# Up products of a feed-forward stage: high and low activations in one matmul of 512 columns, in two halves of a PSUM bank

## The chip, the cores and the metric

One core of one Trainium2 chip runs the whole program. The metric is the device time of one launch in microseconds. Engines are named as in the profile: PE is TensorE (PEld its loads of the stationary operand), DVE is VectorE, ACT is ScalarE, POOL is GpSimd, SP is SyncE.

## What is computed

Two blocks of two layers each on a sequence of 256 tokens with 1024 features. The change touches only the feed-forward part of the first block's layers:

```
def conv_glu_ffn(x, w_up, w_conv, w_down):
    u = causal_dwconv(x @ w_up, w_conv)
    gate, up = jnp.split(u, 2, axis=-1)
    return (jax.nn.silu(gate) * up) @ w_down
...
        h = h + mixed @ w_out[l]
        h = h + conv_glu_ffn(rms_norm(h, norm_ffn[l]), ffn_up[l], ffn_conv[l], ffn_down[l])
```

`w_up` is 1024 x 5632, `w_down` 2816 x 1024, `causal_dwconv` has three taps a column.

## The kernel before, in words

Activations lie transposed, features on the 128 partitions and the 256 tokens along the free dimension. Weights stream from HBM in slabs of 128 x 2048 float32 (1 MB), one slab to a unit of work; three slab buffers and three pairs of split weights rotate. Every product is made from three float32r products: a value is split in a high part (rounded by ScalarE, `act_round`, L566) and the low rest (subtracted by VectorE, `dve_split`, L904), for weights (`w_high`, `w_low`) and activations (`act_high` = `xh`, `act_low` = `xl`) alike, and `gemm` (L1379 to L1384) issues high x high, high x low and low x high, 256 columns each, into the same columns of a PSUM bank.

The order of the work is a list of units (`UNITS_A`) which `woven` turns into one sequence of steps that all engines walk, each doing its own part of a step. Before unit u, ScalarE rounds and VectorE splits the slab of unit u + 2. Round u + 2 waits until the products of unit u - 1 are done, since it writes the same buffer. TensorE begins a unit when `slab_split` has counted its slab.

The feed-forward part has 22 ups and 11 downs. An up (kind `up`, number j) makes one 128-row tile of the gate half and one of the up half: 2 tiles x 8 depths x 3 matmuls = 48. A down takes two hidden tiles into eight output tiles, also 48 matmuls, and adds into banks 3 to 6 over all 11. The order is up 0 to up 5, down 0, up 6, up 7, down 1, and so on to up 20, up 21, down 8, down 9, down 10 (`ffn_units`, `LAG_DOWN = 2`). Ahead of it stand the four `out` units (attention and mixer results into the residual). Up 0 runs for six depths over the end of that, between the sums of squares of the new norm (`sum`, L1494) on TensorE; its factor per token is spread over partitions by one matmul in bank 7 (`pe_spread`, L1538) and copied by ScalarE into the row `ROW_` (`norm` in `scalar_a`, tally `row_kept`).

What `ffn(j)` does for up j on the two other engines is where the change is. On VectorE (`vector_a`): multiply the bank by the row into `UP_` (L1012, which frees the bank, tally `dve_emptied`), multiply silu(gate) by the up half of j - 1 (L1019, `hidden`), take the low part of hidden tile j - 2 (L1004), then, once ScalarE has made the newest tap, add the other two taps of both halves in four dependent operations (L1031). On ScalarE (`scalar_a`): silu of j - 1, high part of hidden j - 2, then the newest tap of both halves from `UP_` (L632 is the helper that records all of these). `Line.settled()` makes an engine wait for its own last operation, `Banks.fill` makes TensorE wait until a bank has been read.

Banks 0, 1 and 2 rotate among the units, one for an up; bank 7 belongs to norms and transposes. The plan is made by a program (`plan`), which counts who empties which bank how often.

## Time and profile before

| | |
|---|---|
| median of 3 runs | 1706.5 us (1704.61, 1706.5, 1706.65) |
| the profiled execution | 1709.35 us |
| its span | 1707.5 us |
| PE busy | 1678.2 us (98% of the span), 13048 matmuls |
| DVE busy | 1165.8 us (68%) |
| ACT busy | 941.9 us (55%) |
| POOL busy | 194.4 us (11%) |
| HBM read | 264.42 MB, 156 GB/s |
| mean granted clock of PE | 0.991 |

The profiled execution is one run on the chip; its 1709.35 us enclose the span, with 1.85 us around it. Shares are of the span. A busy engine is one with at least one instruction in flight; matmuls overlap each other. Line numbers (L1012) are those of the kernel before.

### The profile page before, as it was taken

How to read it: one execution, taken by the hardware profiler on the slowest of the kernel's cores; microseconds unless marked ns; L12 is line 12 of the kernel's file. 1: busy time of each engine (PE TensorE's matmuls, PEld its weight loads, DVE VectorE, ACT ScalarE, POOL GpSimd, SP SyncE). 2: the span in 40 equal slices, each digit the busy share in tenths (PEclk: the TensorE clock that was granted, in tenths of full speed). 3: DMA queues.
4: the chain of work that ended last, by engine and by line, in shares of the span. 5: the costliest groups of instructions: out<-in, count | busy, mean ns of one | idle time of the engine just before them, and what ended most of it. 6: DMA issues, size and time to landing. Idle time of an engine off the chain costs nothing.

```text
span 1707.5 us, 30908 instructions
## 1 busy us (share of the span) xinstructions
PE 1678.2 (98%) x13048; PEld 1533.8 (90%) x13048; DVE 1165.8 (68%) x1627; ACT 941.9 (55%) x1386; POOL 194.4 (11%) x208
## 2 busy tenths in 40 slices
PE   7999999999999999999999999999999999999998
PEld 6989999999998989999999998887888988878887
DVE  7877556787778975548887775656766646567664
ACT  5584425554555574335554555665774556657742
POOL 0454500000001655200000000000000100000000
PEclk9999999999999999999999999999999999999998
DMA  6433533454544424434455554344345453443451
GB/s 226 168 136 105 172 115 124 176 192 176 189 176 168 171 82 137 156 121 168 158 197 180 180 191 168 128 142 162 141 158 187 166 204 124 147 161 137 163 182 50
DMA packets 48058, 268.25 MB, mean 157 GB/s; under 512 B 13553, under 2 KB 14449, under 8 KB 16177
## 3 DMA queue, kind: packets, MB, share of 16 engines
q1 hardware_dynamic: 38448, 264.70, 43.8%
q8 instruction: 104, 1.70, 0.4%
q10 hardware_dynamic: 8704, 0.53, 0.3%
q0 software_dynamic: 768, 1.05, 0.3%
q14 instruction: 34, 0.27, 0.0%
HBM read 264.42 MB, written 1.84 MB: 156 GB/s over the span
## 4 chain that ended last, share of the span: by engine, by line
PE 88%; DVE 7%; ACT 3%; POOL 1%; issue 1%; DMA 0%; SPq 0%; POOLq 0%; DVEq 0%; ACTq 0%
PE bank L1382 14%; PE bank L1383 14%; PE bank L1384 14%; PE bank L2475 10%; PE bank L2477 10%; PE bank L2476 10%; DVE w_low L904 2%; PE bank L2505 2%; ACT arena L632 1%; PE bank L1619 1%; PE bank L2546 1%; PE bank L1620 1%; PE bank L1621 1%; PE bank L2493 1%; DVE arena L1130 1%
## 5 line engine op out<-in xcount | busy, mean ns | idle before, releaser
L904 DVE TENSOR_TENSOR w_low<-slab,w_high 128x2048 fp32r<-128x2048 f32 x250 | 585.2, 2345 | 243.9 <-ACT w_high L566 236.4
L1382 PE MATMUL bank<-act_high,w_high 128*128 128x256 f32 x2304 | 660.1, 287 | 0.1
L1383 PE MATMUL bank<-act_low,w_high 128*128 128x256 f32 x2304 | 652.0, 283 | 0.0
L1384 PE MATMUL bank<-act_high,w_low 128*128 128x256 f32 x2304 | 651.8, 283 | 0.0
L566 ACT ACTIVATE w_high<-slab 128x2048 fp32r<-128x2048 f32 x250 | 474.0, 1897 | 154.1 <-PE bank L2477 88.3
L1382 PEld LDWEIGHTS bank<-act_high,w_high 128*128 128x128 f32 x2304 | 441.9, 192 | 9.0 <-issue 5.9
L1383 PEld LDWEIGHTS bank<-act_low,w_high 128*128 128x128 f32 x2304 | 442.2, 192 | 0.7 <-issue 0.5
L1384 PEld LDWEIGHTS bank<-act_high,w_low 128*128 128x128 f32 x2304 | 442.0, 192 | 0.0
L2475 PE MATMUL bank<-w_high,act_high 128*128 128x512 f32 x768 | 306.3, 399 | 0.0
L2477 PE MATMUL bank<-w_low,act_high 128*128 128x512 f32 x768 | 300.9, 392 | 0.0
L2476 PE MATMUL bank<-w_high,act_low 128*128 128x512 f32 x768 | 300.2, 391 | 0.0
L2477 PEld LDWEIGHTS bank<-w_low,act_high 128*128 128x128 f32 x768 | 144.7, 188 | 31.0
L2475 PEld LDWEIGHTS bank<-w_high,act_high 128*128 128x128 f32 x768 | 145.0, 189 | 29.8 <-issue 1.3
L2476 PEld LDWEIGHTS bank<-w_high,act_low 128*128 128x128 f32 x768 | 145.1, 189 | 28.4
L2036 POOL TENSOR_TENSOR arena<-arena 128x512 f32<-128x512 f32 x9 | 14.7, 1632 | 1318.6 <-ACT arena L581 1318.5
L632 ACT ACTIVATE arena<-bank 128x512 f32<-128x512 f32 (+2 forms) x96 | 47.8, 520 | 133.5 <-PE bank L1384 39.0
L632 ACT ACTIVATE arena<-arena,vectors 128x256 f32<-128x256 f32 x88 | 40.0, 502 | 121.8 <-DVE arena L1012 121.8
L2108 ACT ACTIVATE arena<-bank,small 128x512 f32<-128x512 f32 x80 | 54.8, 685 | 79.4 <-PE bank L2477 78.4
L1031 DVE SCALAR_TENSOR_TENSOR arena<-arena,vectors 128x255 f32<-128x255 f32 (+1 forms) x176 | 85.2, 484 | 13.4 <-ACT arena L632 5.1
L2108 ACT ACTIVATE arena<-arena,small 128x256 f32<-128x256 f32 (+1 forms) x128 | 56.8, 445 | 40.5 <-DVE small L2335 40.5
L632 ACT ACTIVATE act_high<-arena 128x256 fp32r<-128x256 f32 (+1 forms) x68 | 32.6, 482 | 51.3 <-DVE arena L1085 29.4
L632 ACT ACTIVATE arena<-bank,vectors 128x256 f32<-128x256 f32 x64 | 26.4, 472 | 48.8 <-PE bank L1384 48.3
(239 smaller groups left out, 1711.6 us busy)
## 6 DMA issues: line engine op xcount, KB each, us to landing
slab<-stream_a SPq DMA_DIRECT2D x144, 1024.0 KB, 4.8
slab<-stream_b SPq DMA_DIRECT2D x104, 1024.0 KB, 4.8
residual<-x_t SPq DMA_DIRECT2D x4, 256.0 KB, 5.5
lora_weights<-lora SPq DMA_DIRECT2D x2, 512.0 KB, 8.0
out_t<-residual SPq DMA_DIRECT2D x4, 256.0 KB, 2.2
d_inverse<-arena POOLq DMA_DIRECT2D x2, 256.0 KB, 2.7
constants<-common SPq DMA_DIRECT2D x1, 384.0 KB, 9.6
slab<-stream_a SPq DMA_DIRECT2D x2, 160.0 KB, 6.1
```

The lines of the kernel that those rows point to most:

```text
L566: line.did(eng.activation(core.wh[u % PARTS][:, 0:SLAB_WIDTH[u]], core.slab[u % SLABS][:, 0:SLAB_WIDTH[u]], ACT.Copy), core.sem("slab_high"))
L632: line.did(eng.activation(out, in_, func, **kw), tally)
L904: line.did(line.eng.tensor_tensor(core.wl[u % PARTS][:, 0:SLAB_WIDTH[u]], core.slab[u % SLABS][:, 0:SLAB_WIDTH[u]], core.wh[u % PARTS][:, ...
L1031: did(stt(out=out[:, lag:T], in0=src[:, 0:T - lag], scalar=col("conv", 2 * FT * tap + half * FT + j), in1=out[:, lag:T], op0=ALU.mult, op1 ...
L1382: eng.matmul(out, wh, xh, start=first, stop=False, skip_group_check=True)
L1383: eng.matmul(out, wh, xl, start=False, stop=False, skip_group_check=True)
L1384: return eng.matmul(out, wl, xh, start=False, stop=last, skip_group_check=True)
L2108: line.did(eng.activation(out, in_, func, **kw), tally)
L2475: mm(bank[b][:], high, wh[:, k, :], start=(half == 0 and k == 0), stop=False, skip_group_check=True)
L2476: mm(bank[b][:], low, wh[:, k, :], start=False, stop=False, skip_group_check=True)
L2477: last = mm(bank[b][:], high, wl[:, k, :], start=False, stop=(half == 1 and k == 3), skip_group_check=True)
L2505: ins = mm(core.pair[:, p * BLOCK:][:, SPAN[m]], qk[rows_, m * P:m * P + P], qk[rows_, T:T + WIDTH[m]], start=True, stop=True, skip_group_ ...
```

## The change

All ups are made otherwise. The high and low activations become one tensor `act` of [128, 2, 16, 256]. A wide matmul with the stationary tile `w_high` moves both parts of one depth, 512 columns, and writes them side by side into a whole bank; a second matmul, of 256 columns, adds `w_low` x high to the left half. Gate and up tile now have a bank each, so that an up uses two banks: 0 and 1 for even j, 2 and 7 for odd j, and the ups no longer take part in the rotation of banks 0 to 2. Behind it ScalarE copies the right halves of both banks (256 columns each) into the arena at `REST_`, VectorE adds them to the left halves, and then multiplies the sum by the row in place. ScalarE waits for that product before the newest tap. Downs, branch and out units keep `gemm`.

```
@@ -180,8 +180,8 @@
-        self.xh = sb("act_high", [P, 16, T], F32R)
-        self.xl = sb("act_low", [P, 16, T], F32R)
+        self.x = sb("act", [P, 2, 16, T], F32R)
+        self.xh, self.xl = self.x[:, 0], self.x[:, 1]
@@ -195,8 +195,10 @@
-        first, self.pair, self.pair2 = [bank(f"bank{i}") for i in range(3)], bank("bank3", 1024), bank("bank5", 1024)
-        self.bank = first + [pair[:, 512 * i:512 * i + 512] for pair in (self.pair, self.pair2) for i in range(2)] + [bank("bank7")]
+        self.wide = {0: bank("bank0", 1024), 2: bank("bank2", 1024)}
+        self.pair, self.pair2 = bank("bank3", 1024), bank("bank5", 1024)
+        self.bank = [pair[:, 512 * i:512 * i + 512] for pair in (self.wide[0], self.wide[2], self.pair, self.pair2) for i in range(2)]
+        self.bank.append(self.bank.pop(3))
@@ -244,10 +246,14 @@
-        parts = 1 + i if kind in ("q", "w") else 4 if (kind, i) == ("down", FT // 2 - 1) else max(fills, 1)
+        parts = 1 if kind == "up" else 1 + i if kind in ("q", "w") else 4 if (kind, i) == ("down", FT // 2 - 1) else max(fills, 1)
+        if kind == "up":
+            b = 2 * (i % 2)
+            freed[b, reader] = freed.get((b, reader), 0) + 1
+            banks, fills = [(b, reader, freed[b, reader])], 0
...
@@ -685,7 +691,10 @@
                 eng.wait_ge(*sem("products").upto(rows[UA["down", (j - 10) // 2]][3]))
             act(core.xh[:, 8 + (j - 2) % 8, :], core.a(HID_ + (j - 2) % 4)[:, 0], ACT.Copy, sem("hidden_high"))
         if j < FT:
-            emptied(core, eng, rows, UA["up", j])
+            made(core, eng, rows, UA["up", j])
+            rest = core.wide[rows[UA["up", j]][4][0][0]][:].rearrange("p (j n t) -> p j n t", j=2, n=2)[:, :, 1]
+            act(core.a(REST_ + 2 * (j % 2), 2), rest, ACT.Copy, sem("rest_copied"))
+            eng.wait_ge(*sem("up_scaled").next(eng))
             for half in range(2):
                 act(core.a(CV_ + 2 * (j % 2) + half)[:, 0], core.a(UP_ + 2 * (j % 2) + half)[:, 0], ACT.Identity,
                     sem("newest_tap") if half else None, scale=vec[:, VA["conv"] + 4 * FT + half * FT + j:][:, 0:1])
@@ -1009,7 +1018,12 @@
             if j == 0:
                 eng.wait_ge(*sem("row_kept").next(eng))
             b = rows[UA["up", j]][4][0][0]
-            did(tt(core.a(UP_ + 2 * (j % 2), 2), heads(bank[b], T), over(flat(core, ROW_), 2), ALU.mult), sem(f"dve_emptied{b}"))
+            up = core.a(UP_ + 2 * (j % 2), 2)
+            parts = core.wide[b][:].rearrange("p (j n t) -> p j n t", j=2, n=2)
+            eng.wait_ge(*sem("rest_copied").next(eng))
+            did(tt(up, parts[:, :, 0], core.a(REST_ + 2 * (j % 2), 2), ALU.add), sem(f"dve_emptied{b}"))
+            line.settled()
+            did(tt(up, up, over(flat(core, ROW_), 2), ALU.mult), sem("up_scaled"))
         if 1 <= j <= FT:
             i = j - 1
             eng.wait_ge(*sem("silu").next(eng))
@@ -1423,6 +1437,32 @@
+    def up_banks(u):
+        b = rows[u][4][0][0]
+        return b, {0: 1, 2: 7}[b]
+    def wide_product(u, j, k):
+        wh, wl = (w[(first + u) % PARTS][:].rearrange("p (k j m) -> p k j m", k=8, j=2) for w in (core.wh, core.wl))
+        at, out = inputs["up"](rows[u][1], k), core.bank[up_banks(u)[j]]
+        eng.matmul(out[:].rearrange("p (n t) -> p n t", n=2), wh[:, k, j, :], core.x[:, :, at, :], start=k == 0, stop=False,
+                   skip_group_check=True)
+        return eng.matmul(out[:, 0:T], wl[:, k, j, :], core.xh[:, at, :], start=False, stop=k == 7, skip_group_check=True)
+    def up(u, steps):
+        if steps[0] == (0, 0):
+            eng.wait_ge(sem("slab_split").sem, first + u + 1)
+            b, partner = up_banks(u)
+            banks.free(partner)
+            banks.fill(b, "dve")
+            banks.held[partner] = banks.held[b]
+        for j, k in steps:
+            last = wide_product(u, j, k)
+        if steps[-1] == (1, 7):
+            last.then_inc(sem("products").sem, 1)
@@ -1467,7 +1507,7 @@
-            by_depth(u, range(6))
+            up(u, [(j, k) for k in range(6) for j in range(2)])
@@ -1477,8 +1517,11 @@
-        if (kind, i) in (("br2", 0), ("out", 0), ("up", 0)):
-            return by_depth(u, range(6, 8) if u in begun else range(8 // len(rows[u][4])))
+        if kind == "up":
+            return up(u, [(j, k) for k in range(6 * (u in begun), 8) for j in range(2)] if i == 0 else
+                      [(j, k) for j in range(2) for k in range(8)])
+        if (kind, i) in (("br2", 0), ("out", 0)):
+            return by_depth(u, range(8 // len(rows[u][4])))
```

TensorE at the entry of the first layer's feed-forward part, before: `bank0` to `bank2` are the rotating banks, `bank7` the norms' bank; the rows in between are more matmuls of the same kinds.

```order
L1494 MATMUL bank7<-constants,arena 128x1 [waits gathered,dve_emptied7]
L1494 MATMUL bank7<-constants,arena 128x1 x3
L1382 MATMUL bank1<-act_high,w_high1 128x256 [waits x_ready,dve_emptied1,slab_split]
L1383 MATMUL bank1<-act_low,w_high1 128x256
L1384 MATMUL bank1<-act_high,w_low1 128x256
...
L1538 MATMUL bank7<-arena,constants 128x256 [waits rooted_sums,diagonal]
L1382 MATMUL bank2<-act_high,w_high2 128x256 [waits dve_emptied2,slab_split]
L1383 MATMUL bank2<-act_low,w_high2 128x256
L1384 MATMUL bank2<-act_high,w_low2 128x256
```

The same place in the changed kernel, where `bank0` is the tensor of banks 0 and 1 and `bank2` that of banks 2 and 7:

```order
L1537 MATMUL bank2<-constants,arena 128x1 [waits gathered,dve_emptied7]
L1537 MATMUL bank2<-constants,arena 128x1 x3
L1449 MATMUL bank0<-act,w_high1 128x512 [waits dve_emptied0,x_ready,dve_emptied1,slab_split]
L1451 MATMUL bank0<-act,w_low1 128x256
...
L1581 MATMUL bank2<-arena,constants 128x256 [waits rooted_sums,diagonal]
L1449 MATMUL bank2<-act,w_high2 128x512 [waits dve_emptied2,row_kept,slab_split]
L1451 MATMUL bank2<-act,w_low2 128x256
```

Three matmuls have become two. Up 0 waits for bank 0 as well, which was read last in unit out 3 (`dve_emptied0`), and up 1 waits for `row_kept`, ScalarE's copy of the spread norm out of bank 7.

VectorE in up 2 (one split of a slab, then `ffn(2)`), before:

```order
L904 TENSOR_TENSOR w_low2<-slab2,w_high2 128x2048 [waits dve_steps,slab_high]
L1012 TENSOR_TENSOR arena<-bank0,arena 128x512 [waits products]
L1019 TENSOR_TENSOR arena<-arena 128x256 [waits silu]
L1004 TENSOR_TENSOR act_low<-arena,act_high 128x256 [waits hidden_high]
L1031 SCALAR_TENSOR_TENSOR arena<-arena,vectors 128x255 [waits hidden_low,newest_tap]
L1031 SCALAR_TENSOR_TENSOR arena<-arena,vectors 128x254 [waits dve_steps]
L1031 SCALAR_TENSOR_TENSOR arena<-arena,vectors 128x255 [waits dve_steps]
L1031 SCALAR_TENSOR_TENSOR arena<-arena,vectors 128x254 [waits dve_steps]
```

And in the changed kernel:

```order
L913 TENSOR_TENSOR w_low2<-slab2,w_high2 128x2048 [waits dve_steps,slab_high]
L1024 TENSOR_TENSOR arena<-bank0,arena 128x512 [waits rest_copied,products]
L1026 TENSOR_TENSOR arena<-arena 128x512 [waits dve_emptied0]
L1033 TENSOR_TENSOR arena<-arena 128x256 [waits silu]
L1013 TENSOR_TENSOR act<-arena,act 128x256 [waits hidden_high]
L1045 SCALAR_TENSOR_TENSOR arena<-arena,vectors 128x255 [waits hidden_low,newest_tap]
L1045 SCALAR_TENSOR_TENSOR arena<-arena,vectors 128x254 [waits dve_steps]
L1045 SCALAR_TENSOR_TENSOR arena<-arena,vectors 128x255 [waits dve_steps]
L1045 SCALAR_TENSOR_TENSOR arena<-arena,vectors 128x254 [waits dve_steps]
```

One operation of 128x512 stands ahead of the multiplication, waits for ScalarE's copy (`rest_copied`) besides the product, and the multiplication waits for it (its own tally of the freed bank).

## Rows read from the trace of the kernel before

**Rows 1.** The page, chain that ended last: shares of the span by engine.

```profile
PE 88%; DVE 7%; ACT 3%; POOL 1%; issue 1%; DMA 0%; SPq 0%; POOLq 0%; DVEq 0%; ACTq 0%
```

**Rows 2.** Busy us of each engine in one stretch of the first feed-forward part, PEclk, DMA.

```profile
360.00:420.00 60.00, 60.00 (x502) 60.00 (x501) 47.46 (x58) 30.27 (x37) 0.00 (x0) 1.00 0.55 195
```

**Rows 3.** The chain of waits from 360 to 480 us, by line.

```profile
by line: PE bank L1383 33.4%; PE bank L1384 33.4%; PE bank L1382 33.3%
```

**Rows 4.** Timeline of PE, second block: start us, us, engine, line, operation, tensors.

```profile
1025.82 0.39 PE L2475 MATMUL bank<-w_high,act_high 128*128 128x512 f32 x1
...
1030.37 0.39 PE L2477 MATMUL bank<-w_low,act_high 128*128 128x512 f32 x1
```

**Rows 5.** Timeline of PE at up 0 and up 1 of the first layer.

```profile
320.11 0.36 PE L1382 MATMUL bank<-act_high,w_high 128*128 128x256 f32 x1
...
327.07 0.47 PE L1382 MATMUL bank<-act_high,w_high 128*128 128x256 f32 x1
```

**Rows 6.** Timeline of DVE: entry of the first layer's feed-forward part; one of the second's.

```profile
319.68 0.68 DVE L1106 TENSOR_TENSOR residual<-bank,residual 128x512 f32<-128x512 f32 x1
...
327.95 0.69 DVE L1012 TENSOR_TENSOR arena<-bank,arena 128x512 f32<-128x512 f32 x1 [1.40 <-ACT arena L632]
329.62 2.04 DVE L1031 SCALAR_TENSOR_TENSOR arena<-arena,vectors 128x255 f32<-128x255 f32 x4 [0.98 <-ACT arena L632]
...
334.01 0.69 DVE L1012 TENSOR_TENSOR arena<-bank,arena 128x512 f32<-128x512 f32 x1
334.61 0.42 DVE L1019 TENSOR_TENSOR arena<-arena 128x256 f32<-128x256 f32 x1
...
352.20 0.69 DVE L1012 TENSOR_TENSOR arena<-bank,arena 128x512 f32<-128x512 f32 x1
...
362.14 4.50 DVE L904 TENSOR_TENSOR w_low<-slab,w_high 128x2048 fp32r<-128x2048 f32 x2
...
823.72 0.69 DVE L1012 TENSOR_TENSOR arena<-bank,arena 128x512 f32<-128x512 f32 x1 [1.40 <-ACT arena L632]
```

**Rows 7.** Timeline of ACT at the same entry.

```profile
327.46 0.39 ACT L632 ACTIVATE arena<-bank 128x256 f32<-128x256 f32 x1 [1.71 <-PE bank L1538]
...
350.26 0.40 ACT L632 ACTIVATE act_high<-arena 128x256 fp32r<-128x256 f32 x1
```

**Rows 8.** DVE, groups by line and shape: count, busy us, mean ns, idle before.

```profile
L1012 DVE TENSOR_TENSOR arena<-bank,arena 128x512 f32<-128x512 f32 x44 | 30.2, 687 | 25.5 <-PE bank L1384 22.7 <-ACT arena L632 2.8
...
L1031 DVE SCALAR_TENSOR_TENSOR arena<-arena,vectors 128x255 f32<-128x255 f32 x88 | 42.6, 484 | 10.2 <-ACT arena L632 5.1
```

**Rows 9.** Timeline of DVE in the steady part, first up to first up.

```profile
402.32 0.69 DVE L1012 TENSOR_TENSOR arena<-bank,arena 128x512 f32<-128x512 f32 x1 [1.46 <-PE bank L1384]
403.15 0.42 DVE L1019 TENSOR_TENSOR arena<-arena 128x256 f32<-128x256 f32 x1
...
419.61 0.69 DVE L1012 TENSOR_TENSOR arena<-bank,arena 128x512 f32<-128x512 f32 x1 [1.46 <-PE bank L1384]
```

**Rows 10.** ACT, groups by line and shape: the copies out of a bank.

```profile
L632 ACT ACTIVATE arena<-bank 128x512 f32<-128x512 f32 x46 | 26.4, 597 | 62.9 <-PE bank L1384 37.2 <-issue 17.9 <-PE bank L1641 6.2
```

**Rows 11.** Timelines of DVE and PE at the end of the first feed-forward part.

```profile
494.81 0.68 DVE L1012 TENSOR_TENSOR arena<-bank,arena 128x512 f32<-128x512 f32 x1
...
501.79 4.50 DVE L904 TENSOR_TENSOR w_low<-slab,w_high 128x2048 fp32r<-128x2048 f32 x2 [1.38 <-ACT w_high L566]
...
511.56 0.40 PE L1619 MATMUL bank<-w_high,act_high 128*128 128x512 f32 x1
```

**Rows 12.** Timeline of PE: last 40-column matmul, then 512 columns at a lower clock.

```profile
529.95 0.27 PE L1621 MATMUL bank<-w_low,act_high 128*128 128x40 f32 x1
530.06 0.62 PE L1619 MATMUL bank<-w_high,act_high 128*128 128x512 f32 x1
...
533.46 0.49 PE L1621 MATMUL bank<-w_low,act_high 128*128 128x512 f32 x1
```

**Rows 13.** PE in a stretch with gaps: busy us, PEclk, DMA.

```profile
108.00:112.00 4.00, 2.49 (x26) 1.00 0.39 109
```

More of the change, by code:

```diff
@@ L157 @@
 YSQ_ = 34
-CV_, SIL_, HID_, UP_, ROW_ = 30, 34, 36, 40, 44
+CV_, SIL_, HID_, UP_, ROW_, REST_ = 30, 34, 36, 40, 44, 45
 BV_, BO_, BZ_, BG_, BQK_, BX_ = (0, 56), 8, (16, 64), (0, 16), (24, 32), 40
@@ L311 @@
     bonus_made=2, bonus_shifted=1, c_copied=4, chunk_made=8, clamped=1, columns_turned=4, conv_done=4,
-    convolved=22, decay_made=2, decays=1, diagonal=2, dve_emptied0=17, dve_emptied1=16, dve_emptied2=16,
+    convolved=22, decay_made=2, decays=1, diagonal=2, dve_emptied0=21, dve_emptied1=8, dve_emptied2=20,
     dve_emptied3=9, dve_emptied4=5, dve_emptied5=10, dve_emptied6=9, dve_emptied7=7, exps=4, g_made=2,
@@ L317 @@
     newest_tap=22, norm_spread=2, normed=4, off_diagonal=1, outputs_turned=2, products=84, qk_raw=6,
-    queries_ready=1, rate_made=2, reset_made=1, rhs_made=4, rooted=1, rooted_sums=2, roped=6, row_kept=1,
-    sa_made=4, scored=4, silu=22, solved=8, spread_made=4, squared=8, state=3, state_made=3, summed=8,
-    summed_decay=2, tok_made=6, tokens_scaled=1, transposes_in=128, turned=8, u_made=3, weighted=4,
-    x_high=12, x_ready=12, y_made=4, y_rooted=1, y_scale=1, y_squared=2, y_variance=1, ya_done=2, ya_high=2,
-    yb_high=2, yb_ready=2, yc=2, yc_high=2, yc_ready=2, z_mixed=7,), "b": dict(
+    queries_ready=1, rate_made=2, reset_made=1, rest_copied=22, rhs_made=4, rooted=1, rooted_sums=2, roped=6,
+    row_kept=1, sa_made=4, scored=4, silu=22, solved=8, spread_made=4, squared=8, state=3, state_made=3,
+    summed=8, summed_decay=2, tok_made=6, tokens_scaled=1, transposes_in=128, turned=8, u_made=3,
+    up_scaled=22, weighted=4, x_high=12, x_ready=12, y_made=4, y_rooted=1, y_scale=1, y_squared=2,
+    y_variance=1, ya_done=2, ya_high=2, yb_high=2, yb_ready=2, yc=2, yc_high=2, yc_ready=2, z_mixed=7,), "b": dict(
     act_emptied0=9, act_emptied1=8, act_emptied2=7, act_emptied5=16, act_emptied6=17, act_emptied7=16,
```

## Prediction

> **What bounds the kernel now.** I read the page first: TensorE carries 88% of the chain that ended last [rows 1]. That is a whole-span figure, so the next view is busy time by stretch inside the first feed-forward stage (such stages are all that the change touches): TensorE 60.00 of 60 us, VectorE 47.46, ScalarE 30.27, granted clock 1.00 (the 2.4 GHz level) [rows 2]. The chain of waits there is matmuls alone, a third each from the three lines of `gemm` [rows 3]. So a shorter up product shortens the stage, if VectorE, with some 20% free, still delivers in time.
>
> The durations in the rows (0.39 us for a 512-column matmul [rows 4]) mislead here, since matmuls overlap in the pipeline. What a matmul costs is the distance from start to start. From up 1 at 327.07 to the next stage at 511.56 there are 32 units of 48 matmuls of 256 columns [rows 5, 11]: 5.765 us a unit, 0.120 a matmul. In the second block 20 starts of 512 columns lie between 1025.82 and 1030.37, 0.2275 us each [rows 4]. A matmul thus costs its columns at 2.4 GHz (0.107, 0.213) and about 13 to 14 ns more.
>
> **The term that gains.** Per tile and depth, two matmuls of 256 columns and one of 256 (3 x 0.120 = 0.360) become one of 512 and one of 256 (0.2275 + 0.120 = 0.3475). The columns are the same; a matmul's fixed part is saved. Times 16 a unit is 0.20 us (5.56 for 5.765), times 44 units 8.9 us. No row shows the two widths alternating. The nearest rows give the bounds: nothing, if the wide one takes 0.240, and 12.7 ns a group if it costs what the 512-column ones of the second block cost. I take the latter, same type and same size of stationary tile. A loss is excluded by the same number of columns and one load less.
>
> **The terms that lose, in the order of one layer.** (a) Entry of up 0. It needed bank 1; now it needs banks 0 and 1, and bank 0 is read last by the residual add of out 3. That add runs 319.68 to 320.36 [rows 6], TensorE began at 320.11 [rows 5]: it begins at 320.45, 0.34 late. The faster 12 groups win 0.15 of that back before the norm's sums.
> (b) Entry of up 1. Its partner is bank 7, in which the spread norm waits for ScalarE's copy into ROW. TensorE began up 1 at 327.07 [rows 5], the copy runs 327.46 to 327.85 [rows 7] and would be some 0.12 later: up 1 begins at about 328.02, 0.95 late with (a) and the gain of up 0 in it.
> (c) VectorE's backlog. Six ups stand in a row before the first down. One up costs VectorE 6.06 us there (multiplications at 334.01 and, three ups later, 352.20) against 5.765 of TensorE [rows 6]; it falls behind already, covered by some 3 us: the split that up 7 needs ends at 362.14 + 2.29 = 364.43, and up 7 begins at 327.07 + 7 x 5.765 = 367.4. The change adds a dependent 128x512 operation per up: 0.69 us of it [rows 8] and 0.03 between dependent ones (four taps of 484 ns take 2.04) [rows 6, 8], so 0.72. Bounds: 0.60 (an independent operation starts 0.60 after it, 334.01 to 334.61) and 0.83 (402.32 to 403.15) [rows 6, 9]. At up 0 the copy is waited for as well: 0.12 late row, 0.60 for a 128x512 copy out of PSUM [rows 10], 0.72 for the add, 1.4 in all. At the other five it costs nothing: ScalarE ends silu and the high part at 350.66 [rows 7], the copy fits behind them by 351.3, while VectorE is in its split until 352.20 [rows 6]. If that cover were gone each would cost up to 0.65. So the split for up 7 ends 1.4 + 5 x 0.72 = 5.0 later, at 369.45. TensorE alone would be there at 328.02 + 6 x 5.56 + 5.765 = 367.15. **It waits 2.3 us**, first before down 0 (hardly), then before up 6 and up 7, each about 1.1.
> (d) Steady state. Behind that come two ups and a down in turn, 16.9 us of TensorE. VectorE idles in a turn of 17.3 us (402.32 to 419.61), 1.46 of it just before the first up [rows 9], and about as long before the second split after a down, for ScalarE's rounding; 2 x 0.72 goes in, TensorE's turn shrinks by 0.40, and the wait for the copy moves the first multiplication from 0.26 behind the product's end to 1.62. Some 0.9 us stays free. TensorE needs its splits 2.5 and more later, its banks two ups later: nothing.
> (e) Tail. The last up's multiplication comes 2.3 us later after its product than before (1.36 from (d), 0.72 for its own add, 0.20 since the product comes earlier). The split for the last down ends 9.27 after it (494.81; the first of two from 501.79, half of 4.50) at 504.08, and TensorE takes it at 511.56 - 5.765 = 505.8 [rows 11]: slack 1.7, so TensorE waits 0.6. The residual adds and the next stage's first product have 1 us to spare and lose nothing.
>
> **Sum.** Up 7 begins 369.45 for 367.4, 2.05 late with the gains of ups 0 to 6 in it. The 15 ups left win 15 x 0.20 = 3.0, the tail loses 0.6: 0.4 us a layer in favour. The other layer starts alike (its first multiplication at 823.72 waits 1.40 for the copy, as that at 327.95) [rows 6]. Two layers: 0.8 us. The profiled execution takes 1709.35 with a span of 1707.5 and would take 1708.6; it lies 2.85 above the median of 1706.5, so the median comes to **1705.8 us**. What is added elsewhere (44 copies on a ScalarE half idle, the activations in one tensor, other bank addresses) is covered as said or costs no instruction.
>
> **Rivals.** *Slower: the fixed part is not saved.* If the wide matmul costs two narrow ones (0.240), the ups stay at 5.765. Then up 1 begins 1.2 late, the split for up 7 comes at 369.7 against 368.6 (waits 1.1), the tail waits 0.4: 2.7 us a layer, 1711.9 us. It decides below 4 of the 12.7 ns. For it: no row with this pair of widths, and a matmul of only 40 columns is still followed after 0.11 us (529.95 to 530.06) [rows 12], so the load of the stationary tile is nearly as long as a narrow matmul. Against it: the 512-column rows have the same loads and show 0.2275. Chance 0.10. The Trainium skill (TensorE: Matmul & The Clock Gate, "Wait — 56ns, not 53.3ns?") puts the fixed cost of a warm matmul at about 2.5 ns; the trace disagrees, with 13 to 14. By that rule the estimate would be 1710.6, on this rival's side.
>
> *Slower: the clock falls.* Waits of 1.1 us, 5.6 apart, could bring TensorE to 1.2 GHz. The price of a spell: eight matmuls from 530.06 to 533.46 took 0.425 instead of 0.2275 each, 1.6 us [rows 12]. Three or four spells would make about 1711.5. Before that spell TensorE had a run of 40-column matmuls behind it, not an idle gap; between 108 and 112 us it was busy 2.49 of 4 us, less than it would be around such a wait, and the granted clock stayed at 1.00 [rows 13]. Chance 0.08.
>
> *Faster: VectorE's lateness does not reach TensorE.* If the added operation overlapped so well that the split for up 7 came less than 2.7 us late (under 0.3 per up), (c) and (e) vanish: 0.95 - 4.25 a layer, 1699.9 us. The 20% of free time in [rows 2] speaks for it, the contiguous ups in [rows 6], where VectorE has no gap at all, against it. Chance 0.14.
>
> *The change doesn't do what it says:* the order of instructions shows 704 fewer matmuls, 352 a layer, so this is left out.
>
> **Numbers.** The forecast has 0.62. Its own range comes from the bounds of the added operation (0.60 or 0.83: 5 x 0.12 a layer, 1.2 in all), as much again for (a), (b) and (e), and the spread of the three runs (2 us): 1703 to 1709. 0.06 is left for what I don't see, on both sides. The range, 1699.5 to 1710.5, takes in the faster rival and leaves out the two slower ones, 0.18 together. About 0.2%, 3.4 us, is what a measurement of this kernel can tell from no change. Faster by more (under 1703.1): 0.14 and a little of the forecast, 0.20. Slower by more (over 1709.9): 0.20. Within: 0.60.
>
> **What would show it.** Right: the next start 0.2275 behind a wide matmul's and 0.120 behind a narrow one's; TensorE idle 0.3 us before up 0 and 0.9 before up 1; two waits of about 1 us on VectorE's w_low before up 6 and up 7 and one of 0.6 before the last down in each layer, none between; VectorE at about 54 of 60 us in the steady stretch (13.7 + 1.4 of each 16.9), the clock at 1.00 there. Wrong: narrow matmuls longer than 0.120 behind a wide one, waits on w_low in the steady state (then VectorE bounds the stage), or none at all.

## The result, and the profile after

The changed kernel takes 1710.36 us (median of 20 runs, 1708.31 to 1713.5); the kernel before, on the same chip, 1706.97 (20 runs, 1704.19 to 1709.81). The ratio is 1.0016, with an interval of 1.0009 to 1.0023: 2.7 us slower, with a possible 1.5 to 3.9 (the two medians lie 3.4 apart). The forecast was 0.7 us faster. The profiled execution took 1709.08, its span 1707.3. One of all the runs, of the kernel e11 below, took 2647.1 us at a mean granted clock of 0.575; it is in no ratio and no median here.

Both kernels scatter by several us from run to run: TensorE's granted clock falls to its lower level (1.2 GHz) in spells of some us, outside the feed-forward parts. In the profiled executions this happens behind the start, near 110 to 125 us, behind the first feed-forward part, near 605 to 625, behind the second part and at the end, and each execution has it in another selection of these places and for another length. The kernel before spends 32.5 us of its profiled execution so, the changed one 29.3. So one profiled execution cannot be set against another by its span. What compares well is a **feed-forward stretch**: from the first matmul of the norm's sums (behind out 3) to the first matmul of the next stage. All ups and downs lie in it, and the clock is 1.00 throughout. Timeline of PE, kernel before: first and last row of its first stretch, then of its second (start us, us, engine, line, operation, tensors):

```profile
319.23 1.02 PE L1494 MATMUL bank<-constants,arena 128*128 128x1 f32 x8
...
511.56 0.40 PE L1619 MATMUL bank<-w_high,act_high 128*128 128x512 f32 x1
...
814.99 1.02 PE L1494 MATMUL bank<-constants,arena 128*128 128x1 f32 x8
...
1007.34 0.40 PE L2475 MATMUL bank<-w_high,act_high 128*128 128x512 f32 x1
```

192.33 and 192.35 us. The changed kernel, first stretch, with the rows between that the prediction spoke of (in brackets the idle time before the row, and what ended it):

```profile
320.70 1.02 PE L1537 MATMUL bank<-constants,arena 128*128 128x1 f32 x8
322.09 0.47 PE L1449 MATMUL bank<-act,w_high 128*128 128x512 f32 x1 [0.36 <-DVE residual L1120]
...
328.69 0.59 PE L1581 MATMUL bank<-arena,constants 128*128 128x256 f32 x2
329.80 0.47 PE L1449 MATMUL bank<-act,w_high 128*128 128x512 f32 x1 [0.52 <-issue]
...
364.40 0.50 PE L1449 MATMUL bank<-act,w_high 128*128 128x512 f32 x1 [0.34 <-DVE w_low L913]
...
371.20 0.50 PE L1449 MATMUL bank<-act,w_high 128*128 128x512 f32 x1 [0.89 <-DVE w_low L913]
...
508.42 0.38 PE L1396 MATMUL bank<-act,w_high 128*128 128x256 f32 x1 [0.43 <-DVE w_low L913]
...
514.27 0.40 PE L1662 MATMUL bank<-w_high,act 128*128 128x512 f32 x1
```

193.57 us, and 193.49 in the second (817.77 to 1011.26): 1.24 and 1.14 longer, 2.4 in all, which lies within the interval of the measured difference. Outside the two stretches the profiled executions of all kernels of this document take 1318.7 to 1323.6 us, the kernel before 1322.9 and the changed one 1320.2: no loss shows there. The waits are those that were forecast and no others: before up 0, before up 1, before up 6 and up 7, before the last down. In the second layer they stand in the same places, with 0.77 instead of 0.34 before up 6. The chain that ended last has moved with them (page of the changed kernel; [rows 1] before), and in the stretch that stood in [rows 2] VectorE has 54.91 us of work for 47.46:

```profile
PE 81%; DVE 12%; ACT 3%; issue 2%; POOL 1%; DMA 0%; SPq 0%; POOLq 0%; DVEq 0%; ACTq 0%
...
360.00:420.00 60.00, 58.77 (x389) 53.45 (x389) 54.91 (x72) 36.84 (x49) 0.00 (x0) 1.00 0.51 188
420.00:480.00 60.00, 60.00 (x390) 54.43 (x389) 51.68 (x67) 33.26 (x46) 0.00 (x0) 1.00 0.52 193
```

From 420 to 480 us TensorE is never idle. VectorE at the entry has no gaps that would let it catch up: its first operation behind an up's product (timeline of DVE, to be held against [rows 6]) comes every 6.79 us, where it was 6.06.

```profile
337.12 0.69 DVE L1024 TENSOR_TENSOR arena<-bank,arena 128x512 f32<-128x512 f32 x1
337.84 0.69 DVE L1026 TENSOR_TENSOR arena<-arena 128x512 f32<-128x512 f32 x1
...
343.90 0.68 DVE L1024 TENSOR_TENSOR arena<-bank,arena 128x512 f32<-128x512 f32 x1
...
357.48 0.68 DVE L1024 TENSOR_TENSOR arena<-bank,arena 128x512 f32<-128x512 f32 x1
```

What is not as forecast is the matmuls. Timeline of PE in the steady part, and then in the second layer's ups ahead of its first down:

```profile
409.92 0.40 PE L1449 MATMUL bank<-act,w_high 128*128 128x512 f32 x1
410.16 0.28 PE L1451 MATMUL bank<-act,w_low 128*128 128x256 f32 x1
410.27 0.40 PE L1449 MATMUL bank<-act,w_high 128*128 128x512 f32 x1
410.51 0.28 PE L1451 MATMUL bank<-act,w_low 128*128 128x256 f32 x1
...
832.07 0.40 PE L1449 MATMUL bank<-act,w_high 128*128 128x512 f32 x1
832.30 0.28 PE L1451 MATMUL bank<-act,w_low 128*128 128x256 f32 x1
832.42 0.39 PE L1449 MATMUL bank<-act,w_high 128*128 128x512 f32 x1
```

A wide matmul is followed after some 0.236 us, not 0.2275, and the narrow one after 0.117. Over the two ups from 399.67 to 410.62 it comes to **0.353 us a pair** (31 from wide to wide in 10.95) where 0.3475 was forecast and 0.360 was before: 6.7 ns saved and not 12.7. In the second layer's rows the same pair takes 0.35 and less, over a whole up 0.3465 on the average. That pace holds for all 80 pairs from up 1 to the first down of the second layer, the other for the whole first layer and for all later pairs of the second.

### The profile page after: what moved, and what is told of

The parts are those of the page before. It is cut to its first block, busy times and chain, and to the rows that moved or that the text cites. A ratio compares the mean times of both kernels' runs of the same rounds, so it can differ in the third digit from the quotient of the medians.

```text
span 1707.3 us, 29632 instructions
## 1 busy us (share of the span) xinstructions
PE 1673.6 (98%) x12344; PEld 1494.5 (88%) x12344; DVE 1194.5 (70%) x1671; ACT 962.9 (56%) x1430; POOL 191.7 (11%) x208
## 4 chain that ended last, share of the span: by engine, by line
PE 81%; DVE 12%; ACT 3%; issue 2%; POOL 1%; DMA 0%; SPq 0%; POOLq 0%; DVEq 0%; ACTq 0%
PE bank L2518 10%; PE bank L2520 10%; PE bank L2519 10%; PE bank L1396 8%; PE bank L1397 8%; PE bank L1398 8%; PE bank L1449 7%; DVE w_low L913 4%; PE bank L1451 3%; DVE arena L1045 2%; ACT arena L638 2%; PE bank L2548 2%; PE bank L1662 1%; PE bank L1663 1%; PE bank L1664 1%
## 5 line engine op out<-in xcount | busy, mean ns | idle before, releaser
L1396 PE MATMUL bank<-act,w_high 128*128 128x256 f32 x1600 | 460.8, 288 | 0.9 <-DVE w_low L913 0.9
L1397 PE MATMUL bank<-act,w_high 128*128 128x256 f32 x1600 | 453.0, 283 | 0.0
L1398 PE MATMUL bank<-act,w_low 128*128 128x256 f32 x1600 | 452.8, 283 | 0.0
L1396 PEld LDWEIGHTS bank<-act,w_high 128*128 128x128 f32 x1600 | 307.0, 192 | 11.5 <-issue 6.3
L1397 PEld LDWEIGHTS bank<-act,w_high 128*128 128x128 f32 x1600 | 307.2, 192 | 0.6 <-issue 0.5
L1398 PEld LDWEIGHTS bank<-act,w_low 128*128 128x128 f32 x1600 | 307.1, 192 | 0.0
L2518 PE MATMUL bank<-w_high,act 128*128 128x512 f32 x768 | 305.3, 397 | 0.0
L2520 PE MATMUL bank<-w_low,act 128*128 128x512 f32 x768 | 300.0, 391 | 0.0
L2519 PE MATMUL bank<-w_high,act 128*128 128x512 f32 x768 | 299.2, 390 | 0.0
L1449 PE MATMUL bank<-act,w_high 128*128 128x512 f32 x704 | 249.9, 399 | 4.7 <-DVE w_low L913 2.9
L1451 PE MATMUL bank<-act,w_low 128*128 128x256 f32 x704 | 197.4, 280 | 0.0
L638 ACT ACTIVATE arena<-bank 128x512 f32<-128x512 f32 (+2 forms) x140 | 73.4, 541 | 175.3 <-PE bank L1451 39.1
L2520 PEld LDWEIGHTS bank<-w_low,act 128*128 128x128 f32 x768 | 144.2, 188 | 30.9
L2518 PEld LDWEIGHTS bank<-w_high,act 128*128 128x128 f32 x768 | 144.3, 188 | 29.5 <-issue 1.3
L2519 PEld LDWEIGHTS bank<-w_high,act 128*128 128x128 f32 x768 | 144.4, 188 | 28.2
L1449 PEld LDWEIGHTS bank<-act,w_high 128*128 128x128 f32 x704 | 132.3, 188 | 37.9 <-DVE w_low L913 3.9
L1451 PEld LDWEIGHTS bank<-act,w_low 128*128 128x128 f32 x704 | 132.9, 189 | 0.0
```

Of the source, the lines that this page charges most:

```text
L638: line.did(eng.activation(out, in_, func, **kw), tally)
L1396: eng.matmul(out, wh, xh, start=first, stop=False, skip_group_check=True)
L1397: eng.matmul(out, wh, xl, start=False, stop=False, skip_group_check=True)
L1398: return eng.matmul(out, wl, xh, start=False, stop=last, skip_group_check=True)
L1449: eng.matmul(out[:].rearrange("p (n t) -> p n t", n=2), wh[:, k, j, :], core.x[:, :, at, :], start=k == 0, stop=False, skip_group_check=True)
L1451: return eng.matmul(out[:, 0:T], wl[:, k, j, :], core.xh[:, at, :], start=False, stop=k == 7, skip_group_check=True)
```

## The experiments

All kernels ran with their profile, and the table gives what decides: the two stretches, and the kernel's time (median of 5 to 12 runs, of 2 for e12) against runs of the kernel before on the same chip.

| kernel | stretches, us | both against before | median us | ratio [95%] |
|---|---|---|---|---|
| before | 192.33, 192.35 | | | |
| changed (20 runs) | 193.57, 193.49 | +2.4 | 1710.36 | 1.0016 [1.0009, 1.0023] |
| e1_contiguous | 193.68, 193.59 | +2.6 | 1710.78 | 1.0017 [1.0007, 1.0026] |
| e2_no_add | 191.25, 191.24 | -2.2 | 1706.6 | 0.9991 [0.9981, 1.0] |
| e3_row_bank6 | 193.63, 193.72 | +2.7 | 1710.55 | 1.0016 [1.0006, 1.0027] |
| e4_banks_only | 193.61, 193.60 | +2.5 | 1711.4 | 1.0024 [1.0015, 1.0034] |
| e5_tile_order | 192.79, 192.71 | +0.8 | 1710.14 | 1.0012 [1.0, 1.0024] |
| e6_high_first | 190.13, 190.20 | -4.4 | 1704.52 | 0.9979 [0.9969, 0.9989] |
| e7_middle_ups | 190.85, 190.84 | -3.0 | 1707.84 | 1.0001 [0.9992, 1.0011] |
| e8_high_first_from_2 | 189.25, 189.24 | -6.2 | 1702.57 | 0.9975 [0.9963, 0.9987] |
| e9_two_and_two | 192.50, 192.59 | +0.4 | 1706.94 | 0.9995 [0.9984, 1.0006] |
| e10_middle_again | 190.85, 190.86 | -3.0 | 1705.53 | 0.9982 [0.9971, 0.9994] |
| e11_high_first_again | 189.26, 189.26 | -6.2 | 1701.56 | 0.9954 [0.994, 0.9968] |
| e12_add_twice | 201.92, 201.91 | +19.1 | 1728.5 | 1.0117 [1.0099, 1.0135] |

The runs of the kernel before beside them had medians of 1706.97 (changed), 1708.69 (e1 to e4), 1707.6 (e5 to e8) and 1708.63 (e9 to e12). The stretches repeat to 0.1 us, the whole kernel does not repeat to 1.

**Where do the 6 ns of the pair go? e1_contiguous** stores the activations as [128, 16, 2, 256], so that a wide matmul reads one run of 512 columns instead of two of 256.

```
-        self.x = sb("act", [P, 2, 16, T], F32R)
+        self.x = sb("act", [P, 16, 2, T], F32R)
...
-        eng.matmul(out[:].rearrange("p (n t) -> p n t", n=2), wh[:, k, j, :], core.x[:, :, at, :], ...
+        eng.matmul(out[:], wh[:, k, j, :], core.x[:, at].rearrange("p n t -> p (n t)"), ...
```

> Edit: the activation tensor is laid out as 16 tiles x (high, low) x 256 tokens, so that the moving operand of the wide matmul is one run of 512 elements (as in the second block) and not two runs of 256 that lie 16 KB apart. Nothing else. Measured by the feed-forward stretch, from the first sum of squares behind out 3 to the first matmul of the next stage: 192.33 and 192.35 us in the kernel before, 193.57 and 193.49 in the changed one, where a pair of a wide and a narrow matmul took 0.3533 us and not 0.3475. Theory A (the two runs cost the missing 6 ns): a pair takes 0.347 to 0.348; the ups behind the backlog gain 15 x 16 x 5.8 ns = 1.4 us, the tail gives back 0.1: stretch 192.2 to 192.4, time 2.5 us under the changed kernel. Theory B (512 and 256 columns in turn cost it, whatever the layout): pair 0.353, stretch 193.5, time the same.

Nothing moved: the pair still takes 0.353 in the steady part, and the waits are the same within 0.01. The two runs of the moving operand are not the cause.

**e5_tile_order** keeps the matmuls and changes their order in up 1 to up 21.

Here and in e6 and e9 `wide_product` is split in two, and `narrow_product` issues the second matmul.

```
-        for j, k in steps:
-            last = wide_product(u, j, k)
+        runs = [[s] for s in steps] if rows[u][1] == 0 else [steps[0:8], steps[8:16]]
+        for run in runs:
+            for j, k in run:
+                wide_product(u, j, k)
+            for j, k in run:
+                last = narrow_product(u, j, k)
```

> The changed kernel, but in up 1 to up 21 each tile runs its eight 512-column matmuls one behind the other and then its eight 256-column ones, instead of alternating. The same matmuls, banks and waits. Theory A (the missing 6 ns a pair come from the two widths alternating: behind a wide matmul the next one starts 0.236 later, where 512-column ones in a row stand 0.2275 apart): wide ones 0.2275 apart, narrow ones 0.120, 0.3475 a pair. 21 units are then 0.093 us shorter each, of which the waits before up 6 and up 7 take back what lies ahead of them (5 units, 0.5): the feed-forward stretch of a layer is 192.1 us instead of 193.5, the kernel about 1707.5. Theory B (a wide matmul costs 0.236 in this place whatever stands beside it): pair still 0.353, stretch 193.5, kernel 1710. In the changed kernel the ups of layer 1 before the first down ran at 0.3465 a pair and all later ones at 0.353, so two levels exist with the same code.

Timeline of PE in its steady part (rows of one kind are drawn together, xcount at the end):

```profile
399.62 2.00 PE L1449 MATMUL bank<-act,w_high 128*128 128x512 f32 x8
401.46 1.11 PE L1456 MATMUL bank<-act,w_low 128*128 128x256 f32 x8
402.41 2.00 PE L1449 MATMUL bank<-act,w_high 128*128 128x512 f32 x8
```

Eight pairs in 2.79, 0.3488 a pair: the forecast's price was right to some 1 ns for matmuls of one width in a row. The stretch shortened by 0.8, where Theory A gave it 1.4. The waits before up 6 and up 7 grew by 0.40 in the first layer, which Theory A had allowed for with 0.5. What was missing lies behind them: an up takes 5.585 there (379.89 to 391.06 for two) instead of 5.652, so that 15 of them give 1.0 and not 1.4, and the wait before the last down grew by 0.08; the last 0.1 stays open. The kernel was expected at 1707.5 and came at 1710.14, more than its stretches explain; its runs had a mean clock of 0.990 against 0.992 for the kernel before.

**e9_two_and_two** asks whether each change of width has a price.

Against e5:

```
-        runs = [[s] for s in steps] if rows[u][1] == 0 else [steps[0:8], steps[8:16]]
+        runs = [[s] for s in steps] if rows[u][1] == 0 else [steps[n:n + 2] for n in range(0, 16, 2)]
```

> The changed kernel, but the matmuls of up 1 to up 21 come as two of 512 columns, then two of 256, and so on. Theory A (each change of width costs the same, 2.9 ns, and nothing else does: 0.3533 a pair alternating, 0.3488 with eight and eight, 0.348 with sixteen and sixteen): one change of width a pair instead of two, 0.3504 a pair. Theory B (two fixed levels, with the alternation or without it): either 0.353 or 0.348. Stretches 193.0 to 193.2 us under A (21 x 16 x 0.0029 = 1.0 less, of which the waits before up 6 and up 7 take 0.25 back and the last one some).

```profile
399.91 0.39 PE L1456 MATMUL bank<-act,w_low 128*128 128x256 f32 x2
400.14 0.63 PE L1449 MATMUL bank<-act,w_high 128*128 128x512 f32 x2
...
405.48 0.39 PE L1456 MATMUL bank<-act,w_low 128*128 128x256 f32 x2
```

Sixteen pairs in 5.57, 0.3481 a pair, no more than with eight and eight. Theory A of this run falls: a change of width has no price of its own. Of the orders tried only the strict alternation, one and one, has the slower pace, and it has a faster one as well. What makes it fall into the one or the other stays open.

**What do the banks cost? e4_banks_only** leaves the new banks and goes back to the old three matmuls, with no copy and no add.

```
-        eng.matmul(out[:].rearrange("p (n t) -> p n t", n=2), wh[:, k, j, :], core.x[:, :, at, :], ...
...
-        return eng.matmul(out[:, 0:T], wl[:, k, j, :], core.xh[:, at, :], start=False, stop=k == 7, ...
+        return gemm(eng, out[:, 0:T], (wh[:, k, j, :], wl[:, k, j, :]), (core.xh[:, at, :], core.xl[:, at, :]), k == 0, k == 7)
```

> Edit to the changed kernel: each up uses its pair of banks, but is made of the old three matmuls of 256 columns, all into the left half; no copy, no add, nothing left out of the result. This is the bank part of the change alone. Theory A: the entry waits of up 0 and up 1 are paid in full, since here TensorE bounds all that follows and VectorE still has 3 us of slack before up 7: stretch 192.34 + 1.1 to 1.4 = 193.4 to 193.7, time 2.2 to 2.8 us over before. Rival (such a start is made up for later): stretch 192.3 to 192.6.

193.61 and 193.60 for 192.33 and 192.35, with no other wait in them: where TensorE sets the pace, the late begin of up 0 and up 1 costs 1.27 us a layer in full. **e3_row_bank6** takes the wait before up 1 away, by putting the spread norm in bank 6.

```
-            act(flat(core, ROW_), bank[7][:, 0:T], ACT.Copy, sem("row_kept"))
+            act(flat(core, ROW_), bank[6][:, 0:T], ACT.Copy, sem("row_kept"))
...
-    eng.matmul(core.bank[7][:, 0:T], core.const("ones"), flat(core, DIAG_), start=True, stop=True).then_inc(
+    eng.matmul(core.bank[b][:, 0:T], core.const("ones"), flat(core, DIAG_), start=True, stop=True).then_inc(
```

> Edit to the changed kernel: the spread norm is made in bank 6, free at that point, so that up 1 (banks 2 and 7) no longer waits for ScalarE's copy into the row. Theory A (behind the entry VectorE's chain decides, which starts at that copy and not at up 1): up 1 begins 0.9 to 1.1 us earlier, the waits on w_low before ups 5 and 6 grow by as much, the beginning of up 7 relative to the first sum, the stretch (193.5) and the time do not move. Rival (the entry wait adds to the rest): stretch 192.5, time 2 us less.

```profile
327.49 0.59 PE L1581 MATMUL bank<-arena,constants 128*128 128x256 f32 x2
327.73 0.58 PE L1449 MATMUL bank<-act,w_high 128*128 128x512 f32 x1
...
356.43 0.39 PE L1396 MATMUL bank<-act,w_high 128*128 128x256 f32 x1 [0.20 <-DVE w_low L913]
...
363.22 0.50 PE L1449 MATMUL bank<-act,w_high 128*128 128x512 f32 x1 [0.78 <-DVE w_low L913]
```

Up 1 follows the spread norm directly (at 327.73, 8.15 behind the stretch's first matmul; in the changed kernel it is 9.10, 1.11 behind the spread norm), and nothing is won: the stretch is 193.63. TensorE only waits longer later: 0.20 before the first down, 0.78 before up 6 (it was 0.34), 0.89 before up 7, which begins when its w_low is there. The entry's cost and VectorE's backlog cover each other; TensorE pays the larger one up to up 7.

**What does VectorE cost? e2_no_add** leaves out the copy and the add, so that w_high times the low activations is missing from the up products.

```
-            eng.wait_ge(*sem("rest_copied").next(eng))
-            did(tt(up, parts[:, :, 0], core.a(REST_ + 2 * (j % 2), 2), ALU.add), sem(f"dve_emptied{b}"))
-            line.settled()
-            did(tt(up, up, over(flat(core, ROW_), 2), ALU.mult), sem("up_scaled"))
+            did(tt(up, parts[:, :, 0], over(flat(core, ROW_), 2), ALU.mult), sem(f"dve_emptied{b}"))
```

> Edit to the changed kernel: ScalarE's copy of the right halves and VectorE's add are left out, the multiplication reads the left halves; so the high x low part of the up products is not added in. Theory A (VectorE's backlog and the waits at the entry make up what the matmuls don't win): no wait on w_low before up 5, up 6 or the last down is left, the entry of up 0 and up 1 keeps its 1.26 us, 21 ups win 21 x 0.107: stretch 192.34 + 1.26 - 2.25 = 191.35, time 2 us under before and 4.4 under the changed kernel. Rival (VectorE has room, the loss sits elsewhere, in the matmuls or the clock): the stretch stays within 0.5 us of 193.5.

191.25: no wait on w_low is left, though the entry is as late as in the changed kernel. So all three waits on w_low come from the added work (the copy, the add and the waits between them), and with the late entry already paid it costs 193.57 - 191.25 = 2.3 us a layer. Against the kernel before, this one has only the other two terms: the stretch is 1.08 shorter, with 1.27 of entry in it, so the gain of 22 ups is 2.35 us a layer, 0.107 an up. **e12_add_twice** doubles the suspect.

```
             did(tt(up, parts[:, :, 0], core.a(REST_ + 2 * (j % 2), 2), ALU.add), sem(f"dve_emptied{b}"))
             line.settled()
+            did(tt(flat(core, SCRAP_, 2), flat(core, UP_ + 2 * (j % 2), 2), flat(core, REST_ + 2 * (j % 2), 2), ALU.add))
```

> The changed kernel with VectorE's add of 512 columns done twice in each up (the second into a scrap tile). Theory A (a backlog is carried until it is worked off, and the steady state is free only by the 1.5 us that VectorE has left in 17.07): the wait before up 6 and up 7 together grows from 1.2 to about 5.5 us, and a turn of two ups and a down needs VectorE for 17.23 us, so that TensorE waits on w_low in every turn and once more before the last down; stretch about 201.5 us instead of 193.5, kernel +16 us against the changed one. Rival (only the entry counts, steady turns are free): +4.3 us a layer, stretch 197.8.

```profile
353.07 0.47 PE L1451 MATMUL bank<-act,w_high 128*128 128x512 f32 x1 [1.46 <-DVE arena L1024]
...
367.41 0.50 PE L1451 MATMUL bank<-act,w_high 128*128 128x512 f32 x1 [1.51 <-DVE w_low L913]
...
391.90 0.28 PE L1453 MATMUL bank<-act,w_low 128*128 128x256 f32 x1
392.21 0.50 PE L1451 MATMUL bank<-act,w_high 128*128 128x512 f32 x1
...
516.21 0.39 PE L1398 MATMUL bank<-act,w_high 128*128 128x256 f32 x1 [1.61 <-DVE w_low L913]
```

201.92 where Theory A had 201.5: the steady part is over its edge too. The waits up to up 7 come to 5.6 as drawn (1.46, 0.94 before the down, 1.51 and 1.71), forecast 5.5. A turn of two ups and a down takes 17.28 us (VectorE's single split of a turn at 399.60, the next at 416.88) for 17.06 in the changed kernel, and TensorE waits once a turn, as at 391.90 to 392.21 instead of 0.117 later. One thing was not foreseen: now the first wait is for a bank (VectorE's add frees it), not for w_low.

**Can the waits on w_low be avoided? e6_high_first** lets the wide matmuls of an up wait for ScalarE's rounding alone, and the narrow ones, behind all sixteen, for VectorE's split.

```
+            eng.wait_ge(sem("slab_high").sem, first + u + 1)
...
+            for j, k in steps:
+                wide_product(u, j, k)
+            eng.wait_ge(sem("slab_split").sem, first + u + 1)
+            for j, k in steps:
+                last = narrow_product(u, j, k)
```

> The changed kernel, but in up 1 to up 21 all sixteen 512-column matmuls come first and wait for w_high alone (ScalarE's rounding), and the sixteen 256-column ones come behind them and wait for w_low (VectorE's split). This gives VectorE 3.6 us more for each split of an up. Theory A (the waits before up 6, up 7 and the last down are nothing but VectorE's lateness with w_low: 0.34 + 0.89 + 0.43 us in layer 0): the waits before up 6 and up 7 vanish and VectorE's lateness of about 2 us costs nothing; the wait before the last down stays. Stretch 193.5 - 1.2 = 192.3 with the pair at 0.353, and 2.0 less, 190.3, if the matmuls of one width in a row bring 0.3475. Rival: the lateness only moves on to the release of the banks or to the next split, before a down, and the waits come back there: stretch 193.5 (or 191.5).

```profile
399.80 1.72 PE L1456 MATMUL bank<-act,w_low 128*128 128x256 f32 x13
401.36 3.82 PE L1449 MATMUL bank<-act,w_high 128*128 128x512 f32 x16
405.01 1.24 PE L1456 MATMUL bank<-act,w_low 128*128 128x256 f32 x9
```

Sixteen wide matmuls in 3.65, 0.228 each, and the stretch is 190.13 against 190.3 expected. The waits before up 6 and up 7 are gone; VectorE is as late as before and nobody needs it earlier. The one before the last down stays (0.53). This kernel does all the changed one does and is faster than the kernel before.

**e7_middle_ups** gives only up 6 to up 19 the new form (with the layout of e1).

```
+WIDE_UPS = range(6, 20)
...
-        if kind == "up":
+        if kind == "up" and i in WIDE_UPS:
```

> Only up 6 to up 19 take the new form; up 0 to up 5 and up 20 and 21 keep the old one (three 256-column matmuls, their old banks, no copy and no add). Theory A (the change loses at the entry and by VectorE's backlog there, and gains 0.107 us a unit elsewhere, with a pair of 0.353): no wait before up 0 and up 1 beyond those of the kernel before, none before up 6, up 7 and the last down; the stretch is 192.33 - 14 x 0.107 = 190.8 us, the kernel about 1704. Rival 1 (the added VectorE work makes waits in the steady state too once TensorE is not held up at the entry): waits on w_low somewhere in ups 6 to 19, stretch 191.5 or more. Rival 2 (no gain in the pair at all there): 192.3.

Both stretches are 190.8 as expected, 1.5 shorter, with no wait left in them; that is 14 x 0.107. The whole kernel did not show it: 1.0001. **e10_middle_again** is the same kernel again.

> The kernel of e7_middle_ups once more, since its two feed-forward stretches were 1.5 us shorter each and its time was not. Theory A (the 3 us come back as half-speed spells of TensorE outside these stretches: mean granted clock 0.988 to 0.990 in ten of its eleven runs, against 0.992 for the kernel before): ratio again about 1.000, the stretches again 190.85 in any run, and a profiled run at 0.989 shows more windows with a granted clock below 1 than the first one, at 0.994, none of them between up 2 and the last down. Rival (chance in the first eleven runs): ratio 0.998, clock as in the kernel before.

This time the ratio is 0.9982, what 3 us less would give. The same stretches to 0.02 us, in a profiled execution whose mean clock was 0.989, where that of e7 had 0.994. Windows of e7's execution and then of e10's (busy us of PE, PEld, DVE, ACT, POOL, granted clock, DMA share, GB/s), none of them in a feed-forward stretch:

```profile
605.00:610.00 5.00, 3.47 (x29) 2.73 (x29) 2.92 (x7) 4.97 (x10) 3.17 (x5) 1.00 0.62 210
1015.00:1020.00 5.00, 5.00 (x34) 4.53 (x34) 2.14 (x11) 1.25 (x3) 0.00 (x0) 1.00 0.97 405
```

```profile
605.00:610.00 5.00, 3.50 (x18) 2.34 (x17) 2.15 (x5) 4.97 (x9) 3.25 (x5) 0.70 0.60 210
1015.00:1020.00 5.00, 5.00 (x27) 4.52 (x27) 1.63 (x8) 1.12 (x3) 0.00 (x0) 0.66 0.98 388
```

The kernel's 23 runs fall in two groups: 1702.35 to 1703.9 at a clock of 0.994 (6 runs), and 1706.76 to 1710.3 at 0.988 to 0.990 (16 runs; one lies between). The slower group had 10 of 11 runs in e7 and 6 of 12 in e10. Neither theory holds whole: the stretches' gain is real and the spells are real. But that this kernel has more of them than the one before is not shown: the mean clock of all runs was 0.989 against 0.992 beside e7, and 0.991 against 0.991 beside e10.

**e8_high_first_from_2** puts the readings together: up 0 and up 1 in the old form, up 2 to up 21 in the order of e6, with the layout of e1. It was run again as **e11_high_first_again**. Beside the lines of e6 and e7:

```
+WIDE_UPS = range(2, 22)
```

> Up 0 and up 1 keep the old form, up 2 to up 21 take the new one, with all sixteen 512-column matmuls ahead of the sixteen 256-column ones, and the wait for w_low only before the latter. Theory A (entry waits belong to the banks of up 0 and up 1, the later ones to VectorE's lateness with w_low, and both are taken away here): no new waits but perhaps one before the last down (0.4); stretch 192.33 - 20 x 0.107 = 190.2 us with the pair at 0.353, and 192.33 - 20 x 0.20 = 188.3 if one width in a row brings 0.3475. Kernel about 1702.5 or 1699. Rival (VectorE's lateness comes back before the downs or at the banks): 1 to 2 us more than that.

> The kernel of e8_high_first_from_2 once more, beside e10_middle_again on the same chip: stretches 189.25 us, ratio 0.9975, between 0.996 and 0.9985; its profiled run's windows with a granted clock below 1 compared with those of the kernel before. If the spells cost it too, its gain is less than the 2 x 3.1 = 6.2 us of its stretches.

189.25 in four stretches of four: 3.1 less than before each, where 20 x 0.20 without any wait would give 4.0. The wait before the last down (0.52) takes part of the rest, and the pair is 0.348. The profiled executions spend 22.8 us (e8) and 33.2 us (e11) at the lower clock, the kernel before 32.5, so these do not show that the spells cost it more. It is the fastest kernel here, 0.9975 and 0.9954 against the one before. The intervals of the two ratios barely touch, as those of e7 and e10 do, so between 4 and 8 us is what can be said of the whole; the stretches say 6.2.

## Why the prediction was wrong

The forecast was a gain of 0.8 us in the sum; it came to a loss of 2.4 in the stretches. The range of 1699.5 to 1710.5 holds the measured 1710.36 by 0.14 us only, and its upper end was not worked out from the term that failed: that it holds is luck. The steps, for one layer (a start counts from the stretch's first matmul; before: [rows 5, 11], and 367.56 for up 7):

| point of the layer | forecast | measured |
|---|---|---|
| up 1 begins later by | 0.95 | 1.26 |
| up 7 begins later by | 2.05 | 2.17 |
| next stage begins later by | -0.4 | +1.24 |

- **The term that gains failed, by its size.** "The nearest rows give the bounds ... I take the latter": 0.2275 for the wide matmul came from 512-column matmuls in a row, and no row showed the widths alternating. Alternating they take 0.3533 a pair in every up behind the first down, not 0.3475 (e5, e9 and e6: 0.348 to 0.349 as soon as two or more of one width stand together). A unit saves 0.11 us (0.107 by e2 and e4 together), not 0.20. Up to up 7 this costs nothing, since VectorE sets the time there: the second layer's ups ahead of the first down run at 0.3465, and its stretch is only 0.07 shorter. For the 15 ups behind it is 15 x 0.09 = 1.3 us a layer, 2.7 of the 3.2 us by which the forecast is off. That the order sets the price is shown; why the alternation has this pace is not. The value lay inside the bounds; the sign of the result hung on it, and I gave the forecast a range but left the middle between its bounds no chance of its own.
- (a), (b) right in kind, 0.31 short. TensorE is 0.51 late at up 0 (1.39 behind the sums, before 0.88), not 0.34, and up 0 wins 0.08 before the norm's sums, not 0.15. e4 shows the entry at 1.27.
- (c) right: an added operation costs 0.73 (pitch 6.79 for 6.06), forecast 0.72; TensorE waits before up 6 and up 7. From up 1 to up 7 lie 41.40 us, and 39.75 in e2, which waits nowhere between them: 1.65 of waiting (the rows' 0.34 and 0.89 leave out that the last matmul before a wait is drawn longer than its pitch). Forecast 2.3: the slower pair and the later entry bring TensorE there some 0.9 later, and the split itself (to 371.14) comes some 0.2 later than forecast. The forecast's 5.765 a unit is a little off too: up 1 took 5.93 before and the units behind it 5.76, so that up 7 stood at 367.56 and not at 367.4.
- (d) right: no wait from 371.20 to 508.42, VectorE at 54.91 of 60, forecast 54. e12 shows how small the margin is: with one more add TensorE waits in every turn.
- (e) right: 0.43 drawn before the last down, 0.5 in time, forecast 0.6.
- **Rivals.** The slower one, a fixed part that is not saved, had the right place and half of it came true: 6.7 of 12.7 ns. It was to decide below 4 ns, but that was meant for a clear loss; with the forecast's other terms kept, 6.7 ns make -0.4 + 1.3, some 1 us lost a layer. The clock did not fall at the waits: 1.00 in the windows around them. The faster rival (lateness that does not reach TensorE) is false by e2 and e12. The estimate of 1710.6 by the Trainium skill (TensorE: Matmul & The Clock Gate, "Wait — 56ns, not 53.3ns?") is near the measured 1710.36, but not by its rule: a fixed cost of 2.5 ns is not what these traces show, with 0.120 for 256 columns and 0.228 for 512 in e6.

## What to carry to other kernels

Take a matmul's price from rows with the same neighbours, not only with the same shape, and if none exist, forecast from the middle of the bounds. Try matmuls of one width together, and those that need the late operand last: here that order, with the wait moved to the late half, turned the change from 2.4 us lost to 4.4 gained in the stretches. An operation that an engine has room for in the steady state is still paid where units stand without the pause between them, here in the six ups ahead of the first down. And compare stretches between two fixed instructions where the whole kernel scatters more than the effect.

## What was not expected of the hardware

One and the same sequence of alternating matmuls runs at two paces, 0.3533 and 0.3465 us a pair, and keeps the one that it has over many pairs: in the changed kernel the first layer's ups ahead of the first down run at the slower one, the second layer's at the faster; in e1 likewise; in e3 both layers at the faster; in e2 both at the slower. All ups behind the first down run at 0.353, in each of these kernels; e12 has one there, at 386.46, at 0.347. The slower pace is not an even one. In the changed kernel's first layer the pairs take 0.360, 0.350 and 0.350 in turn (from wide to wide), so that one of three costs as much as the three old matmuls; in its second layer, ahead of the first down, they take 0.350 and 0.343 in turn. With two and two, eight and eight or sixteen and sixteen it is 0.348 to 0.349. The cause stays open; no run tried to set it.
